# A third half buffer for the gate and up weights of the experts, in the room of h, the S5 tables and one buffer of gathered rows

## The reference, cut to what matters

```python
lg = xf @ w_router_group + b_router_group        # 4 groups, the best is taken
le = xf @ w_router_expert + b_router_expert      # 8 experts in it, the best two are taken
hg = einsum('nd,edf->nef', xf, w_exp_gate)       # 2048 -> 256 for each expert
hu = einsum('nd,edf->nef', xf, w_exp_up)
act = silu(hg) * hu * comb[:, :, None]
out = einsum('nef,efd->nd', act, w_exp_down)     # 256 -> 2048
```

## Time and profile before

| | us |
|---|---|
| median of 3 runs (1504.54 to 1506.03) | 1504.72 |
| the profiled execution's own time | 1504.55 |
| its span, first to last instruction | 1502.8 |
| PE busy, of the span | 1228.4 (82%) |
| ACT, POOL, DVE busy | 197.2, 261.9, 516.9 |
| share of 16 DMA engines, SP's queue (q1) | 63.9% |
| same, POOL's queue (q0) and ACT's (q10) | 3.6%, 1.0% |
| mean granted TensorE clock | 0.902 of full speed |

### The profile page before, as it was taken

One profiled execution on the slowest core, in us unless ns is written; L12 is line 12 of the kernel. 1 busy time (PEld: TensorE's weight loads), 2 busy tenths in 40 slices (PEclk: granted clock), 3 DMA queues, 4 the chain that ended last, 5 costly groups with the idle time before them and its releaser, 6 DMA issues.

```text
span 1502.8 us, 14892 instructions
## 1 busy us (share of the span) xinstructions
PE 1228.4 (82%) x5972; PEld 676.8 (45%) x5972; DVE 516.9 (34%) x1019; ACT 197.2 (13%) x319; POOL 261.9 (17%) x568
## 2 busy tenths in 40 slices
PE   5789999998998878989979787868877877878625
PEld 2446555555555445656657473323333322333213
DVE  1402574654573673246621423111111111111044
ACT  1312011010211310132210320000000000000012
POOL 3170288881000000021120000100000000000010
PEclk9999999989999889899989868998999988999957
DMA  9997668666584636332123515999999999999442
GB/s 341 367 359 281 223 224 280 233 220 222 176 280 149 237 104 240 126 94 91 57 70 126 210 46 212 419 421 420 411 408 407 395 401 414 403 411 410 202 142 71
DMA packets 140087, 387.02 MB, mean 258 GB/s; under 512 B 15212, under 2 KB 54502, under 8 KB 112559
## 3 DMA queue, kind: packets, MB, share of 16 engines
q1 hardware_dynamic: 132208, 361.91, 63.9%
q0 software_dynamic: 6528, 18.72, 3.6%
q10 hardware_dynamic: 1280, 5.42, 1.0%
HBM read 385.95 MB, written 23.13 MB: 272 GB/s over the span
## 4 chain that ended last, share of the span: by engine, by line
PE 45%; DMA 26%; DVE 10%; POOL 10%; issue 3%; SPq 3%; ACT 2%; DVEq 0%; POOLq 0%; ACTq 0%
DMA slot<-in_w_exp_up 21%; PE psum L1409 10%; PE psum L1066 10%; PE psum L1345 5%; PE psum L1099 4%; DMA slot<-in_w_ada 3%; PE psum L995 3%; PE psum L965 3%; PE psum L956 2%; POOL mem L540 2%; POOL sq L538 2%; POOL sq L541 2%; POOL mem L543 2%; POOL sq L542 1%; POOL sq L539 1%
## 5 line engine op out<-in xcount | busy, mean ns | idle before, releaser
L1409 PE MATMUL psum<-slot,mem 128*64 128x512 f32 x1024 | 255.0, 656 | 86.2 <-DMA slot<-in_w_exp_up 85.3
L1066 PE MATMUL psum<-hT,slot 128*128 128x320 f32 (+1 forms) x1056 | 307.3, 451 | 0.0
L1066 PEld LDWEIGHTS psum<-hT,slot 128*128 128x128 f32 (+1 forms) x1056 | 203.9, 196 | 99.5 <-issue 26.9
L1409 PEld LDWEIGHTS psum<-slot,mem 128*64 128x64 f32 x1024 | 85.6, 151 | 254.1 <-issue 170.0
L2124 DVE TENSOR_TENSOR sq<-sq,psum 128x256 f32<-128x256 f32 x16 | 6.7, 421 | 379.6 <-ACT sq L911 379.6
L965 PE MATMUL psum<-slot,cT 128*8 128x512 f32 (+1 forms) x768 | 102.6, 646 | 22.1 <-DMA slot<-in_w_ada 22.1
L1433 PE MATMUL psum<-mem,sq 128*64 128x512 f32 x512 | 113.4, 594 | 8.7 <-issue 7.1
L610 POOL DMA_INDIRECT moe_output<-mem,idx x16 | 16.2, 1010 | 482.6 <-ACT mem L915 482.6
L1345 PE MATMUL psum<-mem,slot 128*128 128x320 f32 x256 | 71.9, 445 | 5.4 <-DVE mem L1952 5.4
L1099 PE MATMUL psum<-mem,slot 128*128 128x320 f32 x256 | 75.2, 450 | 0.0
L1433 PEld LDWEIGHTS psum<-mem,sq 128*64 128x64 f32 x512 | 41.9, 137 | 69.9 <-issue 68.0
(11 more groups left out here) (423 smaller groups left out, 1316.8 us busy)
## 6 DMA issues: line engine op xcount, KB each, us to landing
slot<-in_w_ada SPq DMA_DIRECT2D x48, 2048.0 KB, 9.9
slot<-in_w_exp_gate SPq DMA_DIRECT2D x64, 1024.0 KB, 13.3
slot<-in_w_exp_up SPq DMA_DIRECT2D x64, 1024.0 KB, 16.5
mem<-in_w_exp_down SPq DMA_DIRECT2D x32, 2048.0 KB, 18.2
slot<-in_w_in SPq DMA_DIRECT2D x17, 2048.0 KB, 11.2
slot<-in_w_out SPq DMA_DIRECT2D x8, 2048.0 KB, 8.2
mem<-in_w_in SPq DMA_DIRECT2D x2, 2048.0 KB, 18.3
mem<-in_x_prompt ACTq DMA_DIRECT2D x1, 2048.0 KB, 11.9
```

The costliest lines, as they stand in the source:

```text
L1066: last = mm(psum[0:wd, grp % 2, 0:T], w[:, k, q * P:q * P + wd], hT[:, k, :], start=(k == 0), stop=(k == KD - 1))
L1409: last = mm(psum[rows_, 0, :].rearrange("p (w n) -> p w n", w=2), xe[i % 2][:, k, rows_], gate_up[h][:, :, k, :], start=(k == 0), stop=(k ...
```

## The change

`slot` is cut another way: each of its four rows is split in two halves, and the halves of all four rows form buffer 0 and buffer 1 of 4 MB. A third buffer of 4 MB, `gu_third`, lies in `mem`. Halves are numbered j = 2i + q and go round the three buffers, each with a semaphore of its own. `hT` and the S5 tables `BDT` and `CT` are moved into `mem` so that the third buffer can lie over them; it also takes the place of one of the two buffers of gathered rows, and of the place where the router weights and the routing's scratch were, which move down.

```diff
         xT = sb("xT", [P, KD, T])
-        hT = sb("hT", [P, KD, T])
         slot = sb("slot", [P, RING, KD * CW])
-        mem = sb("mem", [P, NPROJ * T + NXBC * TPAD + 7808])
+        S5_0 = NPROJ * T + NXBC * TPAD + 7808
+        H0 = S5_0 + 2048
+        mem = sb("mem", [P, H0 + KD * T])
+        hT = mem[:, H0:H0 + KD * T].rearrange("p (k t) -> p k t", k=KD)
...
-        gate_up = [slot[:, 2 * h:2 * h + 2, :].rearrange("p w (k n) -> p w k n", k=KD) for h in range(2)]
+        gu_third = flat[:, 18000:26192].rearrange("p (s n) -> p s n", s=4)
+        gate_up = [slot[:, :, 0:8 * CW], slot[:, :, 8 * CW:16 * CW], gu_third]
+        h2_back = [slot[:, 3, 0:D], slot[:, 3, D:2 * D], flat[:, 18000:18000 + D]]
...
-        xg = [flat[:, 14336 + 2048 * i:16384 + 2048 * i] for i in range(2)]
+        xg = flat[:, 14336:16384]
...
-        wr = flat[:, 18684:18684 + KD * 36].rearrange("p (k e) -> p k e", k=KD)
+        wr = flat[:, 16636:16636 + KD * 36].rearrange("p (k e) -> p k e", k=KD)
...
             for i in range(1, NPAIR):
                 for q in range(2):
-                    sp.wait_ge(S("gu_used"), 2 * i - 1 + q)
+                    if i == 1 and q == 0:
+                        sp.wait_ge(S("hn_turned"), 12)
+                    else:
+                        sp.wait_ge(S("gu_used"), 2 * i - 2 + q)
                     for h in range(2):
                         for w in range(2):
                             load_half(i, h, w, q)
...
+            add_pieces(OUT_PIECES[len(early):])
+
+            pool.wait_ge(S("ssd_done"), NCH)
             pool.dma_start(wr[:, :, 0:4], ...)           # router weights and biases, 4 DMAs
...
-            add_pieces(OUT_PIECES[len(early):])
-
-            pool.wait_ge(S("ssd_done"), NCH)
...
-            for i in range(2):
-                pl(g.memset(xg[i], 0.0))
+            pl(g.memset(xg, 0.0))
...
             for i in range(NPAIR):
-                if i >= 2:
-                    pool.wait_ge(S("xe_turned"), 4 * (i - 1))
+                if i:
+                    pool.wait_ge(S("xe_turned"), 4 * i)
...
-                        pe.wait_ge(S(f"gu_landed{k // 8}"), 64 * (i + 1))
+                        pe.wait_ge(S(f"gu_landed{j % 3}"), 64 * (j // 3 + 1))
```

More of the change, by code:

```diff
@@ L216, in build @@
         sm = sb("sm", [P, 18, 16])
-        BDT = sb("BDT", [P, 2, 4, P])
-        CT = sb("CT", [P, 2, 4, P])
+        BDT, CT = (mem[:, S5_0 + 1024 * i:S5_0 + 1024 * i + 1024].rearrange("p (w u n) -> p w u n", w=2, u=4) for i in range(2))
         dtw = [t[0:NH].rearrange("p w u n -> p (w u n)")[:, T * i:T * i + T] for t in (BDT, CT) for i in range(3)]
@@ L270, in build @@
         aS = flat[:, HQ * T:HQ * T + 3072].rearrange("p (s n) -> p s n", s=6)
[L271 to L272 removed]
+        bnat = mem[:, H0 + 4800:H0 + 4896].rearrange("p (q w h) -> p q w h", q=3, w=2)
         U32 = mybir.dt.uint32
@@ L290, in build @@
         ynat = r1
-        tri = flat[:, 18432:18560]
-        count_i = flat[:, 18592:18656].bitcast(I32)
-        wr = flat[:, 18684:18684 + KD * 36].rearrange("p (k e) -> p k e", k=KD)
-        brow = flat[0:1, 19260:19260 + 36]
-        rt = flat[:, 19296:19296 + 512]
-        comb = flat[:, 19808:19808 + 96].rearrange("p (j e) -> p j e", j=3)
+        tri = flat[:, 16384:16512]
+        count_i = flat[:, 16544:16608].bitcast(I32)
+        wr = flat[:, 16636:16636 + KD * 36].rearrange("p (k e) -> p k e", k=KD)
+        brow = flat[0:1, 17212:17212 + 36]
+        rt = flat[:, 17248:17248 + 512]
+        comb = flat[:, 17760:17760 + 96].rearrange("p (j e) -> p j e", j=3)
         A1, A2, Mk, rk, ge, am = (sq[:, 0, 96 * i:96 * i + 96].rearrange("p (j e) -> p j e", j=3) for i in range(6))
@@ L428, in load_half @@
             def load_half(i, h, w, q):
-                part = slice(8 * CW * q, 8 * CW * (q + 1))
-                sp.dma_start(slot[:, 2 * h + w, part], (gate, up)[w][2 * i + h, :, part])\
-                  .then_inc(S(f"gu_landed{q}"), 16)
+                b = (2 * i + q) % 3
+                sp.dma_start(gate_up[b][:, 2 * h + w, :], (gate, up)[w][2 * i + h, :, 8 * CW * q:8 * CW * (q + 1)])\
+                  .then_inc(S(f"gu_landed{b}"), 16)
             def load_dn(i, h):
@@ L453, in _ @@
                     load_dn(i, h)
-            gate, up = (a[f"w_exp_{x}"][0].rearrange("e (k p) n -> e p k n", p=P) for x in ("gate", "up"))
+            gate, up = (a[f"w_exp_{x}"][0].rearrange("e (p k) n -> e p k n", p=P) for x in ("gate", "up"))
             sp.wait_ge(S("routed"), 6)
             with sp.If(sp.value_load(spill[0:1, :], min_val=0, max_val=2 * T) > 0):
+                sp.wait_ge(S("gu_used"), 2 * NPAIR)
+                for j in range(3):
+                    n = P if j < 2 else TS
+                    sp.dma_start(h2_back[j][0:n, :], h2_dram[j * P:j * P + n]).then_inc(S("x_loaded"), 16)
                 with sp.Fori(1, NE + 1) as e:
@@ L1388, in _, with turn_x @@
             mm(bank(3, 3), ones[:, :], rt[:, 496:499], start=True, stop=True).then_inc(S("rank"), 1)
-            def turn_x(i, g_, par):
-                pe.wait_ge(S(f"xg_landed{par}"), 8 * (i - par) + 16)
+            def turn_x(i, g_):
+                pe.wait_ge(S("xg_landed"), 16 * (i + 1))
                 if 4 * i + g_ >= 2:
@@ L1395, in turn_x @@
                 for q in range(4):
-                    last = tr(bank(6 + g_ % 2, P, lo=q * P), xg[par][:, (4 * g_ + q) * P:(4 * g_ + q + 1) * P], ident[:, :])
+                    last = tr(bank(6 + g_ % 2, P, lo=q * P), xg[:, (4 * g_ + q) * P:(4 * g_ + q + 1) * P], ident[:, :])
                 last.then_inc(S("xe_turned"), 1)
@@ L1404, in hidden @@
                 for k in range(KD):
+                    j = 2 * i + k // 8
                     if k % 8 == 0:
-                        pe.wait_ge(S(f"gu_landed{k // 8}"), 64 * (i + 1))
+                        pe.wait_ge(S(f"gu_landed{j % 3}"), 64 * (j // 3 + 1))
                     for h in range(2):
@@ L1409, in hidden @@
                         last = mm(psum[rows_, 0, :].rearrange("p (w n) -> p w n", w=2), xe[i % 2][:, k, rows_],
-                                  gate_up[h][:, :, k, :], start=(k == 0), stop=(k == KD - 1))
+                                  gate_up[j % 3][:, 2 * h:2 * h + 2, CW * (k % 8):CW * (k % 8 + 1)], start=(k == 0), stop=(k == KD - 1))
                     if k % 8 == 7:
@@ L1439, in _ @@
             for g_ in range(4):
-                turn_x(0, g_, 0)
+                turn_x(0, g_)
             pe.wait_ge(S("routed"), 6)
@@ L1445, in _ @@
                     for g_ in range(3):
-                        turn_x(i + 1, g_, (i + 1) % 2)
+                        turn_x(i + 1, g_)
                 act_turn(i)
                 if i + 1 < NPAIR:
-                    turn_x(i + 1, 3, (i + 1) % 2)
+                    turn_x(i + 1, 3)
                 expert_down(i)
@@ L1469, in _ @@
                 last.then_inc(S("fb_comb_turned"), 1)
+                pe.wait_ge(S("x_loaded"), 32 + 48)
+                for g in range(12):
+                    j, kg = g // 4, g % 4
+                    n = P if j < 2 else TS
+                    if g >= 4:
+                        pe.wait_ge(S("x_transposed"), 12 + g - 3)
+                    for q in range(4):
+                        last = tr(bank(4 + g % 4, n, lo=q * n), h2_back[j][0:n, (4 * kg + q) * P:(4 * kg + q + 1) * P],
+                                  ident[0:n, 0:n])
+                    last.then_inc(S("x_turned"), 1)
+                pe.wait_ge(S("x_transposed"), 24)
                 pe.wait_ge(S("fb_dve"), 2)
@@ L2160, in _ @@
                 v.tensor_copy(combT, psum[0:NE, 3, 0:T]).then_inc(S("fb_dve"), 1)
+                for g in range(12):
+                    j, kg = g // 4, g % 4
+                    n = P if j < 2 else TS
+                    dve.wait_ge(S("x_turned"), 12 + g + 1)
+                    v.tensor_copy(hT[:, 4 * kg:4 * kg + 4, j * P:j * P + n],
+                                  bank(4 + g % 4, 4 * n).rearrange("p (q t) -> p q t", q=4)).then_inc(S("x_transposed"), 1)
                 v.memset(small[:, 62:63], 0.0).then_inc(S("fb_added"), 1)
```

4 lines of the change are left out of this document (2 added, 2 removed).

## The result

The changed kernel takes 1514.21 us (median of 7 runs, 1505.88 to 1515.03), the kernel before 1505.67 us (7 runs, 1504.54 to 1506.61): 0.51% slower, with a 95% interval of 0.32% to 0.70%. The forecast was 4.1 us slower, the measured change is 8.5 us by the medians. The sign and the place were right, the forecast size was half of the measured one, and 1514.2 lies outside the range.

What follows compares the result with a forecast made beforehand. The prediction took expert weight loads, paced by one slowest DMA engine, to bound the kernel. Its terms, 0 - 2.5 + 6.6 = +4.1 us on 1504.55, gave 1508.65, median 1508.8 us; range 1498.5 to 1512.

Steps and rivals of the forecast that it cites:

- (a): Expert stage, steady state: a third half buffer gains 0 us, since the slowest DMA engine is always busy; bounds 0 to -11.5.
- (b): Start of the expert stage: loading pair 1's first half early gains 2.5 us, not the load's 10 us.
- (c): Before pair 0: the early load delays the store of h and so its gather, +6.6 us; bounds 0 and +10.
- (e): Expert stage and fallback: one buffer of gathered rows costs nothing; moved tensors and the longer fallback cost nothing either.
- (d): Ahead of the expert stage: router loads issued later, behind the adds and ssd_done, cost nothing.
- Rival 1: Expert stage: a deeper queue ends the other engines' idle time, up to 11.5 us back, 1497.3 us; chance 0.22.
- Rival 3: Store of h: the four early loads go first, the store ends 10 us later, whole +7.5, 1512.2 us; chance 0.10.
- The signs: Around pair 0 and stage end: later store, gather and down weights, a DMA gap of some 7 us, pace unchanged.

Runs made afterwards that it cites:

- e2: The changed kernel without the early load: pair 1's first half waits for pair 0's first half as before; ratio to the kernel before 1.0018.
- e8: The kernel before without the gathers of pairs 2 to 15; single run, end 509.9 us after the issue of h's store (526.6 before).
- e4: As e1, with the next pair's first half issued ahead of each pair's down weights; ratio to the kernel before 0.9980.
- e1: The changed kernel with the early load of pair 1's first half waiting until pair 0's rows are turned; ratio to the kernel before 0.9995.
- e5: As e1, with pair 2's first half issued ahead of pair 1's down weights, the old order afterwards; ratio to the kernel before 0.9967.
- e6: As e5, with the reload and transposes of h left out of the skipped fallback; ratio to the kernel before 0.9955.
- e9: As e4, with the short fallback of e6; median 1496.84 us beside 1502.79 of the kernel before, ratio 0.9960.
- e3: The changed kernel with the early load waiting until the store of h has landed; ratio to the kernel before 1.0034.
- e7: The changed kernel with half of the early load (2 MB) moved behind pair 0's first half; single run, store of h lands after 16.3 us.
- e10: The changed kernel with the early load 3 us later, behind the routing's second step; single run, store of h lands after 9.5 us.

## Why the prediction was right in kind and wrong in size

- **(a) Room in the steady state, 0 us: right.** 457.0 us against 456.6 between the landings of the first and the last down weights, and e2 without a gain. That the slowest engine paces the stage fits both, but no view here shows the 16 engines one by one, so it stays argued. That indirect traffic is part of its extra work is supported by e8.
- **(b) The early load is worth 2.5 us, not 10: right.** Measured -2.85, with the gap at 945 to 951 us that was foreseen. e4 shows the other 5 us by closing the gap, at the landing of the last half.
- **What failed: the terms behind the collision, put at nothing.** The sum was +4.1 us where the profile shows +9.9. Of the 5.8 us between them 1.4 are the size of (c). Most of the rest are two terms that the sum did not have: +2.05 for a clock that stays at half speed after the longer pause, and +1.2 for the longer fallback. Another 0.9 fall in the final norm, as said above, and 0.55 ahead of the store and ahead of pair 0's first matmul, less 0.35 in (b).
- **The clock: left out.** The hidden layer of pair 0 took 16.0 us instead of 13.95, since the granted clock stayed at half speed until 928.4 us. I had no term for it. The size is partly chance: e1, e5, e6 and e8 show 15.5 us after a pause as short as before, e2, e4 and e9 show 13.95. All four runs with a long pause (the change, e3, e7, e10) lie at 15.9 to 16.2.
- **(e) The longer fallback costs nothing: wrong by 1 us** (e6, e9). The reason given, "no instruction in the executed path changes its shape", was true and not enough.
- **(c) The collision, +6.6 us: too small, and near by luck.** Measured +8.0 at the store. The term was taken from one earlier meeting of the two queues and from equal shares. Both parts of it were off. The late start of the queue that is issued second is missing: 4.1 us instead of 0.9, 3.2 us more. And equal shares were put at +7.5, where they cost some 5: alone the store moved its 2.62 MB from 897.7 to 905 us, at some 360 GB/s, and beside the loads it had half of some 426 GB/s. Late start and half speed together give the measured time: 12.3 us from 901.3 on end at 913.6, and the landing stands at 914.1. The bound of +10 held it.
- **(d) Router loads, and (e) the single gather buffer, nothing: right** (e1, e2).
- **The rivals.** Rival 1, the idle time of the other engines, did not come true in any run with the full traffic. Rival 3 had the size (7.5 us) nearest to what happened, and a part of its mechanism: for 4 us SP's queue had the engines alone. It had a chance of 0.10. With the clock and the fallback left out, the range ended at 1512.
- **The signs.** The store landed at 914.1 us (911 to 913 was said), the down weights of pair 1 were issued at 950.9 (947) and those of pair 15 9.5 us later than before (4). The gap of 6 us and an unchanged pace came as said.

What stays open: which step in starting a DMA makes the second queue late, why in e7 the last 0.08 MB took 3 us, and what, beside the length of the pause, sets when the clock returns and with it the time of the hidden layer of pair 0.

## What to carry to other kernels

A prefetch is worth the idle time that it fills, and only if the queue does not run dry later for another wait: look for the next wait of the issuing engine before counting the bytes. In a stage in which every window shows the DMA engines busy, look first whether the last of several loads on one semaphore lands far behind the others, as here by 9 us: then bytes in flight do not say what PE waits for, and a third buffer brought nothing (e2). And a large load must be kept clear of a small transfer that PE waits for, by waiting until that one has landed: moving one wait took the changed kernel from 8.5 us above the kernel before to 3.1 us below it by the medians (a ratio of 0.9995, so no change that the runs can tell), and only with the later gap moved or closed as well did the runs show it faster (e5, e6, e9; the interval of e4 just reaches no change).

## What was not expected of the hardware

- A transfer that is issued while another queue is at work does not share from the start: its first byte moves 4.1 us (store, in the change and in e7), 5.0 us (loads, in e10) or 4.2 to 4.5 us (gathers, in e10 and e3, and POOL's store in the busy stage before) after its issue. With nothing beside it the store takes 0.9 us and the gather 1.8.
- The delay did not grow with the load in two single profiles: 2 MB and 4 MB beside the store both made it land after 16.3 to 16.4 us, though with 2 MB all but 0.08 MB were over 3 us earlier.
- A block of code that is skipped cost PE 1.0 us more when it was 12 groups of four transposes longer.
- The time at which the granted clock returns after a pause of 7 us varies by some 4 us between runs of nearly the same code: 13.95 or 15.5 us for the same 64 matmul records.
